# Gate and up projections of three feed-forward blocks by Strassen's algebra: pairs of output chunks in seven 256-token products

## What is computed

```python
def swiglu(u, w_gate_up, w_down):            # width 1024 -> 2816 -> 1024
    gate, up = jnp.split(u @ w_gate_up, 2, axis=-1)
    return (jax.nn.silu(gate) * up) @ w_down

def sqrelu_mlp(x, w1, w2):                   # width 1024 -> 4096 -> 1024, twice
    h = jax.nn.relu(x @ w1)
    return (h * h) @ w2
```

## Time and profile before

| | |
|---|---|
| median of 3 runs | 2213.63 us (2213.21 to 2213.8) |
| profiled execution, first to last instruction | 2211.5 us |
| TensorE busy | 2179.2 us, 99% |
| VectorE, ScalarE, GpSimd busy | 1262.7, 855.4, 359.4 us |
| TensorE in the chain that ended last | 94% |
| granted TensorE clock | 0.995 |
| DMA | 187.78 MB, mean 85 GB/s |

### The profile page before, as it was taken

The page is one execution under the profiler, slowest core; times in us unless marked ns, Lnnn a source line. Parts: engine busy times, 40 slices in busy tenths (PEclk is TensorE's granted clock), DMA queues, the critical chain, the costliest instruction groups (busy, mean ns, idle before and its releaser), DMA issues.

```text
span 2211.5 us, 27926 instructions
## 1 busy us (share of the span) xinstructions
PE 2179.2 (99%) x10904; PEld 1730.0 (78%) x10904; DVE 1262.7 (57%) x1953; ACT 855.4 (39%) x1414; POOL 359.4 (16%) x364
## 2 busy tenths in 40 slices
PE   8999999999999999999999999999989999999998
PEld 6888788878888888766688888888865568888886
DVE  5866565654444445487655555566567755555553
ACT  4433464443222224465542222234426753222223
POOL 2301330010000004165310000010136631000001
PEclk9999999999999999999999999999999999999999
DMA  5233125223333332211033333333410013333331
GB/s 173 84 103 95 39 86 172 67 68 95 97 98 98 96 97 86 86 48 48 29 102 98 95 96 95 96 95 118 121 49 1 1 39 95 96 96 96 96 95 48
DMA packets 292659, 187.78 MB, mean 85 GB/s; under 512 B 7856, under 2 KB 286768, under 8 KB 292528
## 3 DMA queue, kind: packets, MB, share of 16 engines
q1 hardware_dynamic: 292240, 185.78, 28.2%
q10 hardware_dynamic: 288, 0.21, 0.0%
HBM read 183.88 MB, written 2.10 MB: 84 GB/s over the span
## 4 chain that ended last, share of the span: by engine, by line
PE 94%; DVE 2%; ACT 2%; issue 1%; DMA 0%; POOL 0%; ACTq 0%; DVEq 0%
PE ps L470 92%; PE ps L504 2%; ACT wh L456 0%; DVE wl L466 0%; DVE tmp L1101 0%; ACT XH L491 0%; ACT p_xscr L654 0%; DMA p_xt<-in_x 0%; DVE sb_small L2937 0%; DVE st_Ll L2297 0%; ACT xb_x L491 0%; DVE H L614 0%; ACT st_L L2249 0%; DVE xb_x L2592 0%; DVE st_L L2281 0%
## 5 line engine op out<-in xcount | busy, mean ns | idle before, releaser
L466 DVE TENSOR_TENSOR wl<-raw,wh 128x1024 fp32r<-128x1024 f32 x336 | 421.6, 1255 | 589.1 <-ACT wh L456 588.7
L456 ACT CAST wh<-raw 128x1024 fp32r<-128x1024 f32 x336 | 349.2, 1040 | 633.0 <-PE ps L470 620.6
L470 PE MATMUL ps<-XH,wh 128*128 128x512 f32 x1072 | 424.9, 396 | 4.7 <-issue 3.6
L470 PE MATMUL ps<-XH,wl 128*128 128x512 f32 x1072 | 418.9, 391 | 0.0
L470 PE MATMUL ps<-XL,wh 128*128 128x512 f32 x1072 | 418.0, 390 | 0.0
L470 PE MATMUL ps<-xb_x,wh 128*128 128x512 f32 x1088 | 339.3, 393 | 0.4 <-DVE H L614 0.3
L557 POOL TENSOR_TENSOR acc<-acc,sq 128x512 f32<-128x512 f32 x55 | 78.6, 1429 | 1320.4 <-ACT sq L547 1319.4
L470 PEld LDWEIGHTS ps<-XH,wh 128*128 128x128 f32 x1072 | 201.2, 188 | 48.3 <-issue 4.7
L470 PEld LDWEIGHTS ps<-xb_x,wh 128*128 128x128 f32 x1088 | 203.1, 188 | 45.0 <-issue 1.1
L470 PEld LDWEIGHTS ps<-XH,wl 128*128 128x128 f32 x1072 | 200.9, 187 | 44.0
L470 PEld LDWEIGHTS ps<-XL,wh 128*128 128x128 f32 x1072 | 201.3, 188 | 41.5 <-issue 0.7
(11 more groups left out here) (397 smaller groups left out, 3452.9 us busy)
## 6 DMA issues: line engine op xcount, KB each, us to landing
raw<-in_mlp_w SPq DMA_DIRECT2D x128, 512.0 KB, 3.7
raw<-in_w_gate_up SPq DMA_DIRECT2D x44, 512.0 KB, 3.7
raw<-in_w_in SPq DMA_DIRECT2D x29, 512.0 KB, 3.7
raw<-in_sb_w_qkv SPq DMA_DIRECT2D x24, 512.0 KB, 3.6
raw<-in_w_down SPq DMA_DIRECT2D x22, 512.0 KB, 3.4
raw<-in_w_out_mix SPq DMA_DIRECT2D x16, 512.0 KB, 3.4
raw<-in_w_kv SPq DMA_DIRECT2D x16, 512.0 KB, 3.7
raw<-in_nsa_w_kv SPq DMA_DIRECT2D x12, 512.0 KB, 3.5
```

The lines of the kernel that those rows point to most:

```text
L456: e.copy(shaped(WH[i % NH], i), shaped(RAW[i % NR], i)).then_inc(*w_hi.up(i))
L466: e.tensor_tensor(shaped(WL[i % NH], i), shaped(RAW[i % NR], i), shaped(WH[i % NH], i).bitcast(F), ALU.subtract).then_inc(*w_lo.up(i))
L470: return e.matmul(out, a, b, start=start, stop=stop, skip_group_check=True)
```

## The change

Two output chunks a and b of a gate or an up projection are now one job. The 512 tokens are two halves of 256, the 1024 inputs are the even and the odd groups of 128, the outputs are a and b: a product of 2x2 blocks, which Strassen's algebra in Winograd's form makes of seven block products instead of eight. Each is 4 groups x 3 matmuls of 256 tokens, in the order p4, p1, p2, p5, p6, p3, p7.

- **Operands of the weights.** From the raw chunks GpSimd makes four sums (`pool_sums`) into two buffers `su`. A pair casts four units instead of two: the odd half of b (`:22`, 512 values wide), a (`:1`), and the two sums (`:12`, `:43`). There are four `wh` and `wl` slots instead of three, and the lookahead is three units. A raw slot is free when its cast and GpSimd's sums are made.
- **Operands of the tokens.** In the projection ahead of a block ScalarE scales each chunk into `tb` (`act_turned_in`), GpSimd makes four combinations of 256 tokens for each two chunks (`pool_combine`), ScalarE and VectorE split them into `tt_t`. The last of the four tiles is split in the block's second job.
- **Out of PSUM.** A pair uses two banks. ScalarE copies p1 with p4, then p5, then p6 to `tp_q` (`act_pair`), and TensorE adds p6, p3 and p7 on top or into the freed halves. VectorE makes the outputs by two sums (`sum_a`, `sum_b`), then scales; the steps of a pair are spread over the jobs behind it.
- **Order.** The first chunks stay single (two gates, or two ups). Then a pair of gates and a pair of ups (SwiGLU), or a pair of ups, with four downs of the group before behind it.
- **Places.** XB holds the input of blocks f and m, the hidden chunks of f and m lie where X is, and the stick-breaking attention reads XB.

```diff
-    NR, NH = 5, 3
+    NR, NH = 5, 4
...
+    def unit_pair(name, ap0, ap1):
+
+        b, a = raw(name + "b", ap1), raw(name + "a", ap0)
+        before = pairs_of.get("last")
+        q0 = operand(name + ":22", "odd", b, [4, 128])
+        q1 = operand(name + ":1", "unit", a, [8, 128])
+        operand(name + ":12", "sum", (name, 0), [8, 128])
+        operand(name + ":43", "sum", (name, 1), [8, 128])
+        raw_done[b] = [(w_lo, (q0,)), (g_made, ("wsum", name, 1))]
+        raw_done[a] = [(w_lo, (q1,)), (g_made, ("wsum", name, 1))]
+        pairs_of[name] = (a, b, q0, before)
+        pairs_of["last"] = name
...
+    def ffn_jobs(gated, groups):
+
+        def pair(g, c):
+            return [("gates", g, c), ("ups", g, c)] if gated else [("ups", g, c)]
+
+        def downs(g, o0, o1):
+            return [("down", g, o) for o in range(o0, o1)]
+
+        last = len(groups) - 1
+        if gated:
+            jobs = [("gate", 0, 0), ("gate", 0, 1), ("ups", 0, 0)]
...
+            jobs = [("up", 0, 0), ("up", 0, 1), ("ups", 0, 2)]
+        for g in range(1, last + 1):
+            c = sum(groups[:g])
+            if g == 1 and not gated:
+                jobs += pair(g, c) + pair(g, c + 2) + downs(0, 0, 8)
+            else:
+                jobs += pair(g, c) + downs(g - 1, 0, 4) + pair(g, c + 2) + downs(g - 1, 4, 8)
+        return jobs + downs(last, 0, 8)
...
+    def sp_weight(e, r):
+
+        if r >= NR:
+            for m, key in raw_done[r - NR]:
+                e.wait_ge(*m.at(*key))
+        e.dma_start(raw_tile(r), RW[r]).then_inc(*w_in[r % NR].up(r))
...
+    def pool_sums(e, name):
+
+        a, b, q0, before = pairs_of[name]
+        ta, tb = raw_tile(a), raw_tile(b)
+        e.wait_ge(*w_in[b % NR].at(b))
+        if before:
+            e.wait_ge(*w_lo.at(UI[before + ":12"]))
+        e.tensor_tensor(SU[0][:, 0:4, :], tb[:, 0::2, :], tb[:, 1::2, :], ALU.add).then_inc(*g_made.up())
+        e.wait_ge(*g_made.now())
+        e.wait_ge(*w_in[a % NR].at(a))
+        e.tensor_tensor(SU[0][:, 4:8, :], SU[0][:, 0:4, :], ta[:, 0::2, :], ALU.subtract).then_inc(
+            *g_made.up("wsum", name, 0))
+        if before:
+            e.wait_ge(*w_lo.at(UI[before + ":43"]))
+        e.tensor_tensor(SU[1][:, 4:8, :], ta[:, 0::2, :], tb[:, 0::2, :], ALU.subtract).then_inc(*g_made.up())
+        e.wait_ge(*g_made.at("wsum", name, 0))
+        e.tensor_tensor(SU[1][:, 0:4, :], ta[:, 1::2, :], SU[0][:, 4:8, :], ALU.subtract).then_inc(
+            *g_made.up("wsum", name, 1))
 
     def mm(e, out, a, b, start, stop):
...
     def pool_xattn(e):
         for o in range(8):
             pool_add(e, "ff", o, act_squared)
+            if o % 2:
+                pool_combine(e, "ff", o // 2)
+            if o == 5:
+                ff.pool_first(e)
...
+    def act_turned_in(e, tag, k, gain):
+
+        j = k // 2
+        if k % 2 == 0 and j:
+            e.wait_ge(*g_made.at("tf", tag, j - 1))
+        e.activation(tb2[k % 2][:, :], H[:, k, :], ACT.Copy, scale=gain).then_inc(*a_made.up("tb", tag, k))
+
+    def pool_combine(e, tag, j):
+
+        e.wait_ge(*a_made.at("tb", tag, 2 * j))
+        e.wait_ge(*a_made.at("tb", tag, 2 * j + 1))
+        if j:
+            e.wait_ge(*x_lo.at("t" + tag, j - 1))
+        b1, b2 = ([t[:, 0:256], t[:, 256:512]] for t in tb2)
+        e.tensor_tensor(tf[:, 0, :], b1[1], b1[0], ALU.subtract).then_inc(*g_made.up())
+        e.wait_ge(*g_made.now())
+        e.tensor_tensor(tf[:, 1, :], b2[1], tf[:, 0, :], ALU.subtract).then_inc(*g_made.up())
+        n = g_made.now()
+        e.tensor_tensor(tf[:, 2, :], b2[1], b1[1], ALU.subtract).then_inc(*g_made.up())
+        e.wait_ge(*n)
+        e.tensor_tensor(tf[:, 3, :], b2[0], tf[:, 1, :], ALU.subtract).then_inc(*g_made.up("tf", tag, j))
+
+    def act_combined(e, tag, j):
+        e.wait_ge(*g_made.at("tf", tag, j))
+        e.copy(TT.hi[:, j, :, :], tf[:, :, :]).then_inc(*x_hi.up("t" + tag, j))
+
+    def dve_combined(e, tag, j):
...
+            self.steps = {n: [] for n in range(len(self.jobs) + 5)}
+            for n, (kind, g, c) in enumerate(self.jobs):
+                if kind[-1] == "s":
+                    quick = kind == "gates" or self.jobs[n + 1][0] != "down" and self.jobs[n + 2][0] != "down" or g == 0
+                    for step, lag in zip(("sum_b", "scale_a", "scale_b", "act_a", "act_b", "low_a", "low_b"),
+                                         (1, 1, 1, 1, 1, 2, 2) if quick else (1, 1, 2, 2, 3, 3, 4)):
+                        self.steps[n + lag].append((step, n))
...
+        def product(self, e, n, part, q, w, out, x, first):
+
+            e.wait_ge(*w_lo.at(q))
+            wh, wl = shaped(WH[q % NH], q), shaped(WL[q % NH], q)
+            for j in range(4):
+                xh, xl = x(j)
+                k = w + j if U[q][0] != "unit" else w + 2 * j
+                mm(e, out, wh[:, k, :], xh, first and j == 0, False)
+                mm(e, out, wh[:, k, :], xl, False, False)
+                f = mm(e, out, wl[:, k, :], xh, False, j == 3)
+            f.then_inc(*proj.up(self.tag, part, n))
+
+        def pe_pair(self, e, n):
+            tag, t = self.tag, "t" + self.norm_tag()
+            A_, C_ = take(e, (tag, "A", n)), take(e, (tag, "C", n))
+            q = self.first(n)
+
+            def block(odd, at):
+                def of(j):
+                    return tuple(x[:, 2 * j + odd, at:at + 256] for x in (self.x.hi, self.x.lo))
+                return of
+
+            def combined(i):
+                def of(j):
+                    e.wait_ge(*x_lo.at(t, j))
+                    return TT.hi[:, j, i, :], TT.lo[:, j, i, :]
+                return of
+
+            def done(i):
+                if not proj.final:
+                    proj.name("unit", q + i)
+
+            self.product(e, n, "p4", q, 0, A_[:, 256:512], combined(3), True)
+            done(0)
+            self.product(e, n, "p1", q + 1, 0, A_[:, 0:256], block(0, 0), True)
+            self.product(e, n, "p2", q + 1, 1, C_[:, 0:256], block(1, 0), True)
+            done(1)
+            self.product(e, n, "p5", q + 2, 0, C_[:, 256:512], combined(0), True)
+            e.wait_ge(*a_made.at(tag, "p1", n))
+            self.product(e, n, "p6", q + 2, 4, A_[:, 0:256], combined(1), False)
+            done(2)
+            e.wait_ge(*a_made.at(tag, "p5", n))
+            self.product(e, n, "p3", q + 3, 0, C_[:, 256:512], block(1, 256), False)
+            e.wait_ge(*a_made.at(tag, "p6", n))
+            self.product(e, n, "p7", q + 3, 4, A_[:, 0:256], combined(2), False)
+            done(3)
+            if not proj.final:
+                proj.name(tag, n)
...
+        def act_pair(self, e, n):
+            tag, q = self.tag, self.first(n)
+            A_, C_ = got((tag, "A", n)), got((tag, "C", n))
+            before = [b for b in range(n) if self.paired(b)]
+
+            act_weights(e, q + 4)
+            e.wait_ge(*proj.at(tag, "p1", n))
+            if before:
+                e.wait_ge(*v_made.at(tag, "sum_a", before[-1]))
+                e.wait_ge(*v_made.at(tag, "sum_b", before[-1]))
+            e.copy(Q4[:, 0:2, :], A_[:, :]).then_inc(*a_made.up(tag, "p1", n))
+            e.wait_ge(*proj.at(tag, "p5", n))
+            e.copy(Q4[:, 3, :], C_[:, 256:512]).then_inc(*a_made.up(tag, "p5", n))
+            e.wait_ge(*proj.at(tag, "p6", n))
+            e.copy(Q4[:, 2, :], A_[:, 0:256]).then_inc(*a_made.up(tag, "p6", n))
+            act_weights(e, q + 6)
 
         def act(self, e, before, after, late=None):
             fence(e, before)
...
+                act_weights(e, self.first(n) + 3)
                 if n == 1:
                     act_root(e, self.norm)
                     act_rs(e, self.norm, self.readers)
+                    act_combined(e, self.norm_tag(), 3)
...
+        def dve_sum_a(self, e, n):
+            tag = self.tag
+            t = take(e, self.tile(n, 0))
+            e.wait_ge(*proj.at(tag, "p3", n))
+            e.wait_ge(*a_made.at(tag, "p6", n))
+            e.tensor_tensor(t[:, :].rearrange("p (a t) -> p a t", a=2), Q4[:, 0::2, :],
+                            got((tag, "C", n))[:, :].rearrange("p (a t) -> p a t", a=2), ALU.add).then_inc(
+                *v_made.up(tag, "sum_a", n))
+
+        def dve_step(self, e, step, n):
+            tag, m = self.tag, int(step[-1] == "b")
+            kind, g, c = self.jobs[n]
+            if step == "sum_b":
+                t = take(e, self.tile(n, 1))
+                e.wait_ge(*proj.at(tag, n))
+                e.wait_ge(*a_made.at(tag, "p5", n))
+                u3 = got((tag, "A", n))[:, 0:256].unsqueeze(1).to_broadcast([128, 2, 256])
+                e.tensor_tensor(t[:, :].rearrange("p (a t) -> p a t", a=2), Q4[:, 1::2, :], u3, ALU.add).then_inc(
+                    *v_made.up(tag, "sum_b", n))
+                return
...
+            if step[:5] == "scale":
+                e.wait_ge(*a_made.at("rs", self.norm))
```

(10 more changed lines are left out.)

324 lines of the change are left out of this document (205 added, 119 removed).

## The result

The changed kernel takes 2216.97 us (median) against 2213.2 for the kernel before: ratio 1.0017, 95% interval 1.001 to 1.0024. It is slower by 3.8 us, which is clear of the noise but within the 0.2% that the prediction called no change. It is 30 us above the forecast of 2187 and outside its range of 2164 to 2207.

What follows compares the result with a forecast made beforehand. TensorE was taken as the bound, busy 2179.2 of 2211.5 us. -53.2 - 1 + 2 + 1 + 9.5 + 6.4 + 8.8 = -26.5 us gave a span of 2185.0 and a median of 2187, range 2164 to 2207.

Steps and rivals of the forecast that it cites:

- The saving: In the pairs, 84 matmuls of 256 tokens at 117.9 ns replace 48 of 512 tokens: 53.2 us less.
- The addresses: Tensors moved to other places let down matmuls gain and query and key matmuls lose a little: 1 us less.
- (b): At each block's start, the first pair's p4 waits for the last combined tile: 2.1 us a block, 6.4 in all.
- (c): In each block's first pair, p6 waits for ScalarE's copy of p1: 2.0, 3.4 and 3.4 us, 8.8 in all.
- the steady part: Past the block starts, back-to-back pairs cost 2 us for late copies and SwiGLU's sums beside VectorE another 1 us.
- (a): At block starts, sum-of-squares matmuls wait for GpSimd's additions, behind combinations and weight sums: 4.5, 3.0, 2.0 us late, 9.5 in all.
- Rival 3: A wait in every pair, p6 behind a queue circle through VectorE: 2238 us at 1 us a pair; chance 0.10.
- Rival 2: The block starts cost little, half of the 25 us of start-up waits going: 2174 us; chance 0.10.
- Rival 5: Nothing much: smaller losses of 0.4 to 0.6 us per pair cancel the gain: 2208 to 2216 us; chance 0.06.
- Weight loads: On TensorE, the skill's rule would hide no full-array load; the prediction held the trace disagrees and charged nothing for loads.

Runs made afterwards that it cites:

- e0: The changed kernel itself, with nothing altered, measured a second time for an undisturbed profile: 2217.0 us, ratio 1.0016 to the kernel before.
- e14: Changed kernel with GpSimd's first weight sums and last combination moved later, and ScalarE's root and VectorE's diagonals ahead of their weight casts: 2206.0 us, ratio 0.9965.
- e10: Changed kernel with each block's first group plain, combined tokens' casts and low halves moved into the block, root and first pair's copies earlier: 2179.7 us, ratio 0.9846.

## Why the prediction was wrong

**The saving** (-53.2): right. 117.7 ns and 9.89 us for a pair, against 117.9 and 9.90.

**The addresses** (-1): the downs run at 227.5 ns where they were 229.1, the direction of the forecast. Whether it is the address was not tried.

**(b) The last combined tile** (+6.4): about right. TensorE waits 5.0 us for `tt_t`, three times, at most 1.8.

**(c) The first copy of p1** (+8.8) **and the steady part** (+3): about right in sum, not in place. Of the 9.9 us of waits for `tp_q` only 2.88 and 2.83 are the first pairs' of the second and third block, where (c) had 3.4 each. The 2.0 of the first block did not come. There the third pair waits 3.46, at the kind of place that the steady part priced at 0.4.

From the first pair on, the distances between starts beyond 117.9 and 228.9 ns sum to 8.5, 7.3 and 7.6 us in the three blocks, 23.4, against 18.2 for (b), (c) and the 3 of the steady part. 15.6 of them are waits, and the rest is mostly matmuls at the lower clock behind them.

**(a) The sum of squares** (+9.5): the step that failed. The time from the start of a block to its first pair grew by 34.8 us. The small matmuls come 10.2, 9.4 and 2.4 us later in their block than before, 22.1 us where the sum had 9.5. Behind them lie another 12.7 us, for which the sum has no term. Its rows for GpSimd were right as far as they go: it had 13.9 us from the addition of chunk 5 to the end of the last one, and e0 shows 15.0 to 15.3. But it let that addition start where it stood before. In e0 it starts 4.6 and 5.2 us later in the first two blocks, measured from the block's first matmul. The sum followed one queue and left out what the others do to it:
- VectorE's low halves of combined tiles, added ahead of the H additions, wait for ScalarE, which waits for GpSimd. The prediction asked what is queued behind each wait inside a pair, and never in the loop ahead of the block. The last H addition comes 9.1 us late in the first block, and with the H additions come late the squares that GpSimd adds.
- The mark that opens the block for ScalarE and VectorE stands behind GpSimd's last combination, and the root stands behind a cast that needs a weight sum.
- The diagonals take 2.75 to 2.83 us instead of 0.87 beside GpSimd's weight sums, in all three blocks. The prediction took "a little" for contention, and only on GpSimd.

The lower clock behind these waits was not foreseen either. At the starts e0's rows show no cost of it, as said above; inside the first pairs it is a part of the 23.4 us.

The sum made with the measured parts closes: -53.2 - 1 + 34.8 + 23.4 = +4.0, against a measured 2215.7 - 2211.5 = +4.2. The first two terms are the forecast's own.

**The rivals.** Rival 3, the slower side, named the right kind of thing (a queue circle through VectorE) and the wrong place: pairs in the steady part never closed it. Rival 2 had the starts cost half of the forecast's 25 us; they cost 58.2 with what the steady part had. Rival 5 had the right number, 2216, by luck: its small losses in every pair did not occur.

**Weight loads.** 84 loads of 188 ns run in a pair of 9.89 us, so the rule that the prediction took from the Trainium skill (TensorE: Matmul & The Clock Gate, Part 3) is not borne out here either. The same part of that page also lets a load into a background weight buffer run ahead of matmuls in flight, which the prediction left out; no run here tells which it is.

## What to carry over

When a change adds work to queues ahead of a block that has no slack, price the block's start as a chain over all queues: for every added instruction, which later instruction of its queue is late, and which engine's opening wait (a fence, a mark) now includes it. Taking one late chain out tells little while another ends beside it; look at which wait took its place. Price VectorE's passes beside GpSimd from rows in which both are busy. And behind a wait look at TensorE's granted clock: what it costs there depends on whether a later wait covers it (nothing to be seen at e0's starts, 3.7 and 4.5 us in e14).

The algebra itself pays: with the first group of each block plain, and the tokens' making ordered by who waits for it (e10), it gives 1.5%.
